# A hybrid recurrence and expert layer on one core: head outputs with tokens on the partitions, earlier loads of the first two experts, six chunks ahead

## The reference, cut to what matters

```python
a = modulate(rmsnorm(x, norm1_g), sh1, sc1)           # adaLN from c (latents) or c_ctx (context)
q, i, z_fwd, z_bwd, g = split(a @ w_in, 5)             # 8 heads of 128
f = lb + (1 - lb) * sigmoid(z);  k = 1 - f             # per direction
# per head and direction, chunks of 64 tokens:
#   S_t = diag(f_t) S_{t-1} + k_t v_t^T ;  o_t = S_t^T q_t     (state carries from context into latents)
o = o_fwd + o_bwd
o = o * rsqrt(mean(o*o over the head's 128 values) + eps) * norm_g * silu(g)
h = x + g1 * (o @ w_out)
ff = modulate(rmsnorm(h, norm2_g), sh2, sc2)
logits = ff @ router_w + router_b;  top 4 of 32, softmax over the four
# expert: z = ff @ w1[e] + b1[e] (1024 -> 2048), clamped SwiGLU, @ w2[e] + b2[e] (1024 -> 1024)
out = rmsnorm(h + g2 * sum of weighted expert outputs, final_g)
```

## Time and profile before

| | before |
|---|---|
| median of 3 runs | 1658.03 us |
| the profiled execution | 1658.75 us |
| its span | 1656.6 us |
| PE busy | 1504.4 us (91%) |
| DVE busy | 731.5 us (44%) |
| ACT busy | 265.3 us (16%) |
| moved by DMA | 497.14 MB, 300 GB/s over the span |

### The profile page before, as it was taken

How to read it: one execution, slowest core, us unless ns; L and a number is a source line. 1 busy time by engine, 2 the same in 40 slices (tenths; PEclk the granted TensorE clock), 3 DMA queues, 4 the chain that set the end, 5 groups by cost and what they waited for, 6 DMA issues and landing times.

```text
span 1656.6 us, 40828 instructions
## 1 busy us (share of the span) xinstructions
PE 1504.4 (91%) x14616; PEld 752.4 (45%) x14616; DVE 731.5 (44%) x2458; ACT 265.3 (16%) x443; POOL 217.2 (13%) x265
## 2 busy tenths in 40 slices
PE   5999999999995997999799799989788979898897
PEld 3668888888653232434243234434232424333233
DVE  4404877666647432434244244434242424343344
ACT  4403555555322000000000000000000000000001
POOL 1000000000152111111011112111111111111110
PEclk9999999999997998999899899999898979999998
DMA  8684111112438998966979989999899989999788
GB/s 359 199 262 138 52 51 51 51 51 55 162 150 330 405 418 362 372 272 259 415 318 403 417 328 397 413 417 400 362 376 417 415 363 365 417 410 416 316 324 321
DMA packets 130870, 497.14 MB, mean 300 GB/s; under 512 B 15372, under 2 KB 48492, under 8 KB 94908
## 3 DMA queue, kind: packets, MB, share of 16 engines
q1 hardware_dynamic: 122588, 479.99, 73.4%
q0 software_dynamic: 8256, 16.81, 2.7%
HBM read 484.92 MB, written 17.58 MB: 303 GB/s over the span
## 4 chain that ended last, share of the span: by engine, by line
PE 60%; DMA 19%; SPq 13%; DVE 4%; issue 3%; ACT 1%; POOL 0%; DVEq 0%; POOLq 0%; ACTq 0%
PE ps L1760 21%; PE ps L1798 11%; DMA big_b<-in_moe_w 9%; DMA arena<-in_moe_w 8%; SPq L430 7%; PE ps L1458 6%; PE ps L1460 5%; PE ps L1459 5%; SPq L424 3%; PE ps L1636 2%; PE ps L1583 1%; PE ps L1570 1%; PE ps L1481 1%; DMA ring_t<-in_mod_c 1%; PE ps L1579 1%
## 5 line engine op out<-in xcount | busy, mean ns | idle before, releaser
L1760 PE MATMUL ps<-arena,rows 128*32 128x512 f32 x2728 | 329.6, 619 | 34.1 <-DMA arena<-in_moe_w 30.1
L1760 PE MATMUL ps<-big_b,rows 128*32 128x512 f32 x2688 | 319.7, 610 | 28.6 <-DMA big_b<-in_moe_w 28.5
L860 ACT ACTIVATE rows<-ps 128x256 f32<-128x256 f32 x84 | 32.4, 386 | 1054.8 <-PE ps L1784 1021.9
L1760 PEld LDWEIGHTS ps<-arena,rows 128*32 128x32 f32 x2728 | 86.9, 112 | 230.0 <-issue 155.2
L1798 PE MATMUL ps<-big_b,rows 128*32 128x256 f32 x2688 | 169.1, 401 | 20.3 <-DMA big_b<-in_moe_w 20.3
L1760 PEld LDWEIGHTS ps<-big_b,rows 128*32 128x32 f32 x2688 | 84.7, 111 | 221.9 <-issue 151.7
L1798 PE MATMUL ps<-arena,rows 128*32 128x256 f32 x2688 | 167.3, 399 | 16.4 <-DMA arena<-in_moe_w 16.4
L1376 DVE SCALAR_TENSOR_TENSOR y_sb<-ps,w_s,g_q 128x256 f32<-128x256 f32 x42 | 20.3, 484 | 251.7 <-PE ps L1798 251.7
L1376 DVE SCALAR_TENSOR_TENSOR rows<-ps,w_s,g_q 128x256 f32<-128x256 f32 x42 | 20.3, 484 | 239.8 <-PE ps L1798 239.8
L1798 PEld LDWEIGHTS ps<-big_b,rows 128*32 128x32 f32 x2688 | 83.7, 114 | 85.7 <-DMA big_b<-in_moe_w 29.6
L1798 PEld LDWEIGHTS ps<-arena,rows 128*32 128x32 f32 x2688 | 83.8, 114 | 79.7 <-DMA arena<-in_moe_w 24.9
(11 more groups left out here) (365 smaller groups left out, 1840.2 us busy)
## 6 DMA issues: line engine op xcount, KB each, us to landing
arena<-in_moe_w SPq DMA_DIRECT2D x192, 1024.0 KB, 16.4
big_b<-in_moe_w SPq DMA_DIRECT2D x192, 1024.0 KB, 14.9
ring_t<-in_hg_w_in SPq DMA_DIRECT2D x32, 512.0 KB, 4.0
ogT<-in_mod_w SPq DMA_DIRECT2D x16, 1024.0 KB, 5.1
arena<-yrows SPq DMA_DIRECT2D x8, 1024.0 KB, 11.9
x_sb<-in_x SPq DMA_DIRECT2D x2, 2048.0 KB, 7.9
arena<-in_hg_w_in SPq DMA_DIRECT2D x4, 1024.0 KB, 25.6
arena<-in_mod_c SPq DMA_DIRECT2D x4, 1024.0 KB, 22.3
```

The costliest lines, as they stand in the source:

```text
L1760: last = mm(bank[q * G:(q + 1) * G, :], XT[par][:, pos * G:(pos + 1) * G], w[:, :, q * NW:(q + 1) * NW], start=(pos == 0), stop=False)
```

## The change

Three things change.

1. Outputs of a head have tokens on the partitions: the decayed queries (64 tokens) and the masked scores become the stationary operand, states and values the moving one. The squares are summed by a DVE reduction along the row into four columns, Ln and Exp work on those four, DVE scales the bank's rows by them, PE turns the rows back by four transposes behind section zf of the next head, and DVE applies gain and gate from PSUM in one operation. The projection's product with g1 is written back to its PSUM bank.
2. Buffers are laid out anew (`lfq` and `gs` in the upper half of the arena, the input rows in two alternating buffers of the ring, `late` for what was in the ring or behind the tokens), and the loads of the first experts move: five chunks of stream 1 after the last head's gate copy, four of stream 0 after its scores, and so on. The w2 of stream 1 is loaded before the loop. The rows of tile 3 come from DVE.
3. AHEAD is 6 and stream 0's chunks lie in order.

```diff
-AHEAD = 5
+AHEAD = 6
-        f_sb = aT_t[:, 0:LT * D].rearrange("p (i n) -> p i n", i=LT)
+        f_two = ring_t[:, 2 * D:4 * D].rearrange("p (i n) -> p i n", i=2)
...
+            for pos in (5, 6, 7, 1, 2):
+                load_w1(1, 1, pos)
+            sp.wait_ge(S["a_ps"], H)
+            for pos in range(W1C // 2):
+                load_w1(0, 0, pos)
             sp.wait_ge(S["o_ps"], H)
             sp.wait_ge(S["og_ok"], H)
-            for pos in range(W1C):
+            for pos in range(W1C // 2, W1C):
                 load_w1(0, 0, pos)
+            sp.wait_ge(S["bias_ok"], 1)
+            load_w1(1, 1, 0)
             for i in range(LT - 1):
-                sp.wait_ge(S["f_ok"], i + 1)
                 store(i)
             sp.wait_ge(S["yo_ps"], 2 * LT)
             for k in range(2):
                 load_w2(0, 0, k)
...
             sp.wait_ge(S["lg_ps"], LT)
             for pos in range(3, 5):
                 load_w1(1, 1, pos)
+            store(LT - 1)
+            load_w2(0, 0, 2)
+            sp.wait_ge(S["h_st"], 16 * LT)
+            for k in range(2):
+                load_w2(1, 1, k)
+            sp.wait_ge(S["ring_free"], 1)
+            load_w2(0, 0, 3)
             for k in range(2, W2C):
-                load_w2(0, 0, k)
-            sp.wait_ge(S["frow_st"], 16 * LT)
-            for pos in range(5, W1C):
-                load_w1(1, 1, pos)
+                load_w2(1, 1, k)
             sp.wait_ge(S["tab_ok"], 1)
             n_pairs = sp.value_load(tab_n[0:1, 0:1], min_val=1, max_val=NPAIR_MAX)
-            sp.wait_ge(S["h_st"], 16 * LT)
-            sp.wait_ge(S["ring_free"], 1)
...
-                A(osb, ps[5][:, :], ACT.Copy).then_inc(S["o_ev"], 1)
                 A(sq, ps[5][:, :], ACT.Square).then_inc(S["sq_ok"], 1)
...
-                A(sq, ps[6][:, :], ACT.Ln, bias=eps_t[:, :], scale=1.0 / P).then_inc(S["rs_ok"], 1)
-                A(sq, sq, ACT.Exp, scale=-0.5).then_inc(S["rs_ok"], 1)
+                act.wait_ge(S["ss_ok"], h1)
+                A(rs4[:, :], ss4[:, :], ACT.Ln, bias=eps_t[:, :], scale=1.0 / P).then_inc(S["rs_ok"], 1)
+                A(rs4[:, :], rs4[:, :], ACT.Exp, scale=-0.5).then_inc(S["rs_ok"], 1)
...
+            def squares(h1):
+                dve.wait_ge(S["sq_ok"], h1)
+                V.tensor_reduce(ss4[:, :], sq.rearrange("p (n v) -> p n v", n=LT), AX_X, ALU.add).then_inc(S["ss_ok"], 1)
+            def normed_rows(h1):
+                dve.wait_ge(S["rs_ok"], 2 * h1)
+                V.tensor_tensor(osb.rearrange("p (n v) -> p n v", n=LT),
+                                ps[5][:, :].rearrange("p (n v) -> p n v", n=LT),
+                                rs4[:, :].unsqueeze(2).broadcast_to([P, LT, P]), ALU.mult).then_inc(S["on_ok"], 1)
             def gate(h1, ho):
-                gla.link(V.scalar_tensor_tensor(osb, osb, g_col, sq, ALU.mult, ALU.mult))
-                V.tensor_tensor(ogT[:, ho, :], osb, gs, ALU.mult).then_inc(S["og_ok"], 1)
+                dve.wait_ge(S["oT_ps"], h1)
+                V.scalar_tensor_tensor(ogT[:, ho, :], ps[6][:, :], g_col, gs, ALU.mult, ALU.mult).then_inc(S["og_ok"], 1)
...
                 V.tensor_copy(v_h, xv[:, :, bass.ds(h * P, P)])
+                if prev is not None:
+                    squares(h)
                 decays(h, 1)
                 if prev is not None:
-                    gate(h, prev)
-                    dve.wait_ge(S["og_ok"], h)
-                dve.wait_ge(S["gm_ok"], h + 1)
-                V.tensor_copy(gs, sgg).then_inc(S["gs_ok"], 1)
+                    normed_rows(h)
                 for d in range(2):
+                    if d == 1:
+                        if prev is not None:
+                            gate(h, prev)
+                            dve.wait_ge(S["og_ok"], h)
+                        dve.wait_ge(S["gm_ok"], h + 1)
+                        V.tensor_copy(gs, sgg).then_inc(S["gs_ok"], 1)
...
-                me.link(V.tensor_tensor(tmp, ps[YO_BANK[j]][:, :], g1_row[:, c0], ALU.mult))
+                me.link(V.tensor_tensor(y, y, g1_row[:, c0], ALU.mult))
...
             V.tensor_copy(msk16[:, :, :], msk).then_inc(S["msk_ok"], 1)
+            f_shifted(LT - 1)
...
-            me.mark(V.memset(tab_nf[:, 1:2], 1.0))
+            me.mark(V.memset(tab_nf[:, 1:2], 0.0))
...
-                        mm(ps[5][:, n * P:(n + 1) * P], v_h[:, CT + n, :], pm[d][:, n, :],
+                        mm(ps[5][:, n * P:(n + 1) * P], pm[d][:, n, :], v_h[:, CT + n, :],
...
-                        last = mm(ps[5][:, ch * CH:(ch + 1) * CH], st[d][:, ch, :],
-                                  lfq[d][:, CTX + ch * CH:CTX + (ch + 1) * CH], start=False,
+                        r = slice((ch % 2) * CH, (ch % 2) * CH + CH)
+                        last = mm(ps[5][r, (ch // 2) * P:(ch // 2 + 1) * P],
+                                  lfq[d][:, CTX + ch * CH:CTX + (ch + 1) * CH], st[d][:, ch, :], start=False,
...
-                mm(ps[6][:, :], ones[:, :], sq, start=True, stop=True).then_inc(S["ss_ps"], 1)
+                for n in range(LT):
+                    last = tr(ps[6][:, n * P:(n + 1) * P], osb[:, n * P:(n + 1) * P], ident[:, :])
```

More of the change, by code:

```diff
@@ L103, in build @@
         sgk = [take(TOK) for _ in range(2)]
-        lfq = [take(TOK) for _ in range(2)]
         bc = [take(TOK) for _ in range(2)]
+        ko = [take(TOK) for _ in range(2)]
         qe = [take(LAT) for _ in range(2)]
         ke = [take(LAT) for _ in range(2)]
-        ko = [take(TOK) for _ in range(2)]
-        qs, sgq, sgg, gs = (take(LAT) for _ in range(4))
+        qs, sgq, sgg = (take(LAT) for _ in range(3))
+        assert at[0] <= 8192
+        at[0] = 8192
+        lfq = [take(TOK) for _ in range(2)]
+        gs = take(LAT)
         pm = [take(LAT).rearrange("p (a t) -> p a t", a=LT) for _ in range(2)]
@@ L176, in build @@
         i8f = rtake(LT * 8).rearrange("p (i e) -> p i e", i=LT)
-        oh = rtake(LT * TOPK * E).rearrange("p (i k e) -> p i k e", i=LT, k=TOPK)
-        ohd = rtake(LT * TOPK * E).rearrange("p (i k e) -> p i k e", i=LT, k=TOPK)
+        oh, ohd = (late[:, n * 512:n * 512 + 512].rearrange("p (i k e) -> p i k e", i=LT, k=TOPK) for n in range(2))
         msk = rtake(LT * E).rearrange("p (i e) -> p i e", i=LT)
@@ L447, in _ @@
                 load_w2(0, 0, k)
-            sp.wait_ge(S["bias_ok"], 1)
-            sp.wait_ge(S["h_ok"], 2 * LT)
-            load_w1(1, 1, 0)
-            sp.wait_ge(S["f3_ok"], 1)
-            store(LT - 1)
-            for pos in range(1, 3):
-                load_w1(1, 1, pos)
             sp.wait_ge(S["lg_ps"], LT)
@@ L627, in _ @@
                 scatter(par)
-            pool.wait_ge(S["fx_ok"], 1)
-            pool.wait_ge(S["ld_mrow"], 16 * 7)
-            me.link(pool.tensor_tensor(f_sb[:, LT - 1, :], f_sb[:, LT - 1, :], G2_row, ALU.mult))
-            pool.tensor_tensor(f_sb[:, LT - 1, :], f_sb[:, LT - 1, :], sh2_row, ALU.add).then_inc(S["f3_ok"], 1)
-            pool.wait_ge(S["frow_st"], 16 * LT)
+            for n in range(2):
+                pool.wait_ge(frow[n], 16 * (LT // 2))
             for par in range(2):
@@ L1021, in states @@
             def states(h1):
-                gla.base, gla.count = 17 * (h1 - 1), 0
+                gla.base, gla.count = 16 * (h1 - 1), 0
                 dve.wait_ge(S["b_ps"], h1)
@@ L1129, in _ @@
                             ALU.mult).then_inc(S["rw_ok"], 1)
+            squares(H)
+            normed_rows(H)
             gate(H, H - 1)
@@ L1576, in outputs @@
                 pe.wait_ge(S["st_ok"], h1)
-                for d in range(2):
-                    for n in range(LT):
-                        mm(ps[5][:, n * P:(n + 1) * P], v_h[:, CT + n, :], pm[d][:, n, :],
+                for n in range(LT):
+                    for d in range(2):
+                        mm(ps[5][:, n * P:(n + 1) * P], pm[d][:, n, :], v_h[:, CT + n, :],
                            start=(d == 0 and n == 0), stop=False, skip_group_check=True)
@@ L1669, in _ @@
             out_part(0, 0, H - 2)
+            turned_back(H - 1)
             pe.wait_ge(S["qs_ok"], H)
@@ L1686, in _ @@
             out_part(3, 0, H - 1)
-            sum_squares(H)
             pe.wait_ge(ld_wout[1], 16)
             pe.wait_ge(S["rw_ok"], 2)
-            for j in range(4, 6):
-                out_part(j, 0, H - 1)
+            out_part(4, 0, H - 1)
+            turned_back(H)
+            out_part(5, 0, H - 1)
             pe.wait_ge(S["og_ok"], H)
```

81 lines of the change are left out of this document (41 added, 40 removed).

## The result

The changed kernel took 1640.78 us (median of 4 runs, 1637.18 to 1646.33); the kernel before, run beside it, 1659.72 (4 runs, 1657.12 to 1663.95). The ratio is 0.9882, with a 95% interval of 0.9860 to 0.9904: 19 us faster, where 22.7 were forecast. The profiled execution took 1641.11 us with a span of 1638.9; its own difference to the span before, 1656.6, is 17.7 us, and that is the number that the traces have to explain.

What follows compares the result with a forecast made beforehand. PE bounds the heads and the loop between expert changes, transfers bound the changes. Front 13.5, early loads 2.2 and six chunks ahead 7 sum to 22.7 us off 1658.03: 1635.3, stated as 1636; range 1624 to 1648, likeliest case 1630 to 1641.

Steps and rivals of the forecast that it cites:

- the likeliest case: Whole kernel: the forecast itself, 1636 us within 1630 to 1641, chance 0.52.
- State products: Head outputs on PE: 32 records overlap in two output halves, 1.7 us instead of 3.52; bounds 1.15 and 3.5.
- rival A: Head outputs or their chain give less: weight loads exposed at 90 ns a record, or DVE's chain longer; 1644 us, chance 0.21.
- Head, in sum: Heads: 2.0 us less for each of six, last head's chain 0.7 longer, 2.2 less behind it; front 13.5 us earlier.
- Behind the heads: Projection and routing up to the loop: tile 3's shift on DVE and its later store cost +1.0 us, bounds 0.3 and 2.5.
- Early loads: Start of the expert loop: 36 loads remain instead of 40, 10.6 us less transfer, but only 2.2 us gained.
- the route's +1.0: Routing ahead of the loop: 1.0 us later through tile 3's shift on DVE and its store, counted within the early loads' 2.2.
- Six ahead: Expert loop's stall groups: one more chunk of PE work before w2, 0.86 us a group, 7 us in all, bounds 0 and 10.
- The loop in sum: Expert loop: first to last L860 sigmoid shrinks by some 10 us, from 1063.3 to about 1053.
- C: Expert loop: the sixth chunk pushes w2 back, each of 12 groups waits 2.64 us longer; slower, 1674 us, chance 0.05.
- D: Start of the loop: tile 3's late store, the gather and PE's low clock cost 15 us; about no change, chance 0.04.
- B: Expert loop gives more: shorter waits keep PE's clock up, up to 2 us in five groups; 1626 us, chance 0.18.

Runs made afterwards that it cites:

- the repetition: The changed kernel run once more as it is, against the kernel before: 1643.50 us (4 runs), ratio 0.9897.

## Why the prediction was right, step by step

The time, 1640.78 us, lies in the range, at the upper edge of the likeliest case's own (1630 to 1641); the repetition, 1643.50, lies past that edge. The heads came as worked out. Behind them errors of several microseconds met, and that they nearly cancelled ahead of the loop is luck.

- **State products: right.** 1.7 us were forecast within 1.15 and 3.5; they take 1.97. The mechanism, overlap of the two halves of the output, is shown by undoing it (3.33 us). The rule of the Trainium skill ("TensorE: Matmul & The Clock Gate", Part 3: a weight load overlaps matmuls in flight only when the row group differs) doesn't describe this case: the row group is the same in both orders, and only the output half changes, yet a record takes 61 or 104 ns; the measurement decides. By the time alone rival A, 1644, would hardly fall (1640.78, and 1643.50 in the repetition); it falls by the 61 ns of a record, where it had 90, and by PE waiting at neither the scores nor the transposes of a head in the loop.
- **Head, in sum: right.** 2.0 us were counted; from scores to scores it is 1.92, so six heads gave 11.5 where 12.0 were said. Up to its scores the last head grew by 0.4 us (0.7 forecast), behind them 1.9 came off (2.2 forecast), and the first head came 0.3 later, which was not counted: 12.7 in all where 13.5 was said.
- **Behind the heads: right in size, wrong in its parts.** +1.0 was forecast and +1.4 came. But it is the difference of two larger numbers, neither of which I had: the mask 3.4 us further ahead, mostly because POOL left DVE alone, and the gather late behind the store of tile 3, which stands behind two loads in the queues. From the mask on, the shift of tile 3 costs 0.5, the late gather 4.2 and the way from the first chunk product to the first sigmoid 0.1: -3.4 + 0.5 + 4.2 + 0.1 = +1.4. (Moving the store gave 3.8 by the traces, and 3.9 to 7.0 between the medians, which hold other things too.) I had the late store at "up to 1 us more", and the ease for DVE not at all.
- **Early loads: too small.** 2.2 us were forecast, with the route's +1.0 and the sixth chunk's 0.86 in it, so some 4 of their own. Undoing them costs 4.4 to 6.5 us in the loop with six ahead and 6.7 with five; why more than 4 is open. The first refill came at 546.63, 10.85 us earlier than before, where 559.7 - 13.5 = 546.2 was forecast. The stretch after the first sigmoid moved data at

```profile
536.00:650.00 114.00, 98.51 (x1120) 34.86 (x1116) 40.71 (x186) 3.46 (x9) 17.10 (x17) 0.93 0.92 374
```

  a DMA share of 0.92 instead of 0.98: the transfers removed there no longer fill it.
- **Six ahead: the step that was mis-sized.** 7 us were forecast; the runs showed 2.0 to 4.1 (with early loads), 4.4 (with late ones) and 5.3 (in the kernel before) in the loop. Behind it PE does one more chunk that nobody needs, 0.86 us that I had not counted; in the sum of that stretch it is lost in the scatter. Net this makes 1.1 to 4.4; the one pair of medians that tells it from nothing says 2.3, with an interval of the ratio from 0.9963 to 0.9997. What ate the rest is in the sums over the loop: I had waits end earlier by a whole chunk in most groups, but only the waits for w2 fell, and those for the chunks, in most traces with the chunks' own time, grew by most of that.
- **The loop in sum.** The distance was to shrink by some 10 us and shrank by 7.55. Early loads and the sixth chunk do not add up: together they give less than the sum of what each gives alone. In us from first to last sigmoid (the same kernel traced twice differs by up to 1.8):

| | five ahead | six ahead |
|---|---|---|
| late loads | 1063.28, 1065.01 | 1057.97, 1060.65 |
| early loads | 1058.27 | 1054.14 to 1056.26 |

- **The rivals.** C, slower, needed w2 behind six w1 loads to end the stalls. The waits on w2 fell instead, from 36.7 us (16.4 and 20.3) over the loop to 29.1 (13.8 and 15.3), and those on w1 rose from 58.6 to 62.6. Even with seven ahead w2 is waited for less (21.6 us); what made that kernel slower is another thing. D occurred in small: the late store, not 15 us but some 4. B (more from the loop) did not occur.

## What to carry to other kernels

- With 64 weight columns, order the products so that successive ones write the two halves of the output's partitions; the same records in the other order cost 1.4 us for 32.
- Where loads are brought forward, look at what stands behind them in the queues: here a 0.5 MB store ahead of two 1 MB loads instead of behind them was worth 3.8 us, where all the early loads were worth 4.4 to 6.7.
- A parameter that gave something from 5 to 6 can lose from 6 to 7 by a mechanism that has nothing to do with the first: look at the steps without stalls as well.

## What the runs showed of the hardware

- DVE's elementwise work waits for POOL's beside it: four 128x128 comparisons of f32 in SBUF take 0.90 us alone and 3.04 or 3.05 beside a 128x1024 addition on POOL, where one of the four takes 2.43 us and the others stay at 0.28 to 0.29; a cast of 128x32 takes 0.18 or 0.92.
- The slowing depends on the moment. Four 32x32 copies that begin 1.5 us behind POOL's first bias instruction took 1.53 us (three traces), 1.6 to 2.3 us behind it 3.19 to 3.21 (five, the kernel before among them), 3.3 to 5.2 us behind it 6.22, 6.23, 7.96 and 7.97. Where they took over 6 us, the products ahead of the last head's new state products waited 1.7 to 2.5 us, against 0.65 in the others. In the longest case (7.97 us) one copy alone took 3.94, beside a POOL subtraction of 4.08. It may be a cause of the spread between runs of the same kernel, up to 9 us: the traced executions with copies over 6 us took the longest of their kernel in three cases of four. That is not shown by an experiment.
- Waiting can cost twice: behind the waits of a stall group the w2 phase takes up to 5.7 us (5.74 at a granted clock of 0.63) instead of 3.66 at 1.00; in other traces the same phase took as little as 3.66.
